# Cached keys of the samples turned by VectorE in 32x32 blocks, and loaded by quadrants in pieces of 128 bytes

## What is computed

```python
k_past = cache_k[l][page_table].reshape(dec_batch, past_len, N_KV_HEADS, HEAD_DIM)
k_all = jnp.concatenate([k_past.astype(k.dtype), k], axis=1)
...
qg = q.astype(F32).reshape(b, t, N_KV_HEADS, N_HEADS // N_KV_HEADS, HEAD_DIM)
s = jnp.einsum('btkgd,btnkd->btkgn', qg, kg) * (HEAD_DIM ** -0.5)
p = jax.nn.softmax(s, axis=-1)
o = jnp.einsum('btkgn,btnkd->btkgd', p, vg)
```

## Time and profile before

| | us |
|---|---|
| median of 3 runs | 3478.99 |
| the three runs | 3478.44, 3482.11, 3478.99 |
| span of the profiled execution | 3480.9 |
| PE busy | 3402.1 (98%) |
| POOL busy | 1224.1 (35%) |
| DVE busy | 1815.1 (52%) |
| ACT busy | 1058.5 (30%) |
| mean granted TensorE clock | 0.992 |

### The profile page before, as it was taken

The page is one execution under the profiler, slowest core; times in us unless marked ns, Lnnn a source line. Parts: engine busy times, 40 slices in busy tenths (PEclk is TensorE's granted clock), DMA queues, the critical chain, the costliest instruction groups (busy, mean ns, idle before and its releaser), DMA issues. The chain is left out here.

```text
span 3480.9 us, 66517 instructions
## 1 busy us (share of the span) xinstructions
PE 3402.1 (98%) x27598; PEld 3177.2 (91%) x27598; DVE 1815.1 (52%) x2545; ACT 1058.5 (30%) x1464; POOL 1224.1 (35%) x508
## 2 busy tenths in 40 slices
PE   5899999999999999999999999999999999999999
PEld 2699989889999989998888999898999998999999
DVE  1523578979986123332325245888889841242201
ACT  2322332223542334222213222322245423332221
POOL 0243333436323223333333433334362332233433
PEclk9899999999999999999999999999999999999999
DMA  9834434656545774658895656544332257744442
GB/s 327 278 108 115 114 105 121 182 172 199 158 131 163 232 241 157 211 194 290 293 294 171 185 170 179 142 123 111 104 115 74 87 186 234 231 140 137 124 130 88
DMA packets 559562, 593.12 MB, mean 170 GB/s; under 512 B 74780, under 2 KB 524593, under 8 KB 549179
## 3 DMA queue, kind: packets, MB, share of 16 engines
q1 hardware_dynamic: 559260, 588.86, 55.4%
HBM read 546.37 MB, written 116.39 MB: 190 GB/s over the span
## 5 line engine op out<-in xcount | busy, mean ns | idle before, releaser
L858 POOL TENSOR_TENSOR w_lo_t<-raw,w_hi_t 128x1024 fp32r<-128x1024 f32 x472 | 1179.0, 2498 | 2233.5 <-ACT w_hi_t L871 2233.5
L1177 PE MATMUL acc<-act_hi,w_hi_t 128*128 128x272 f32 x6528 | 1392.6, 295 | 21.7 <-POOL w_lo_t L858 11.8
L1177 PE MATMUL acc<-act_hi,w_lo_t 128*128 128x272 f32 x6528 | 1354.1, 289 | 0.0
L1177 PE MATMUL acc<-act_lo,w_hi_t 128*128 128x272 f32 x6528 | 1350.1, 288 | 0.0
L1177 PEld LDWEIGHTS acc<-act_hi,w_hi_t 128*128 128x128 f32 x6528 | 1029.0, 189 | 92.7 <-issue 70.5
L1177 PEld LDWEIGHTS acc<-act_lo,w_hi_t 128*128 128x128 f32 x6528 | 1029.1, 189 | 0.0
L1177 PEld LDWEIGHTS acc<-act_hi,w_lo_t 128*128 128x128 f32 x6528 | 1023.5, 190 | 0.0
L871 ACT ACTIVATE w_hi_t<-raw 128x1024 fp32r<-128x1024 f32 x472 | 499.9, 1059 | 1611.2 <-PE acc L1177 1598.3
L1765 DVE SCALAR_TENSOR_TENSOR conv<-conv,cw 128x512 f32<-128x512 f32 x240 | 241.4, 1006 | 38.8 <-POOL w_lo_t L858 38.8
L1177 PE MATMUL acc<-m_hi,w_hi_t 128*128 128x272 f32 x1024 | 215.8, 292 | 0.0
L1177 PE MATMUL acc<-m_lo,w_hi_t 128*128 128x272 f32 x1024 | 211.5, 288 | 0.0
(11 more groups left out here) (248 smaller groups left out, 2623.1 us busy)
## 6 DMA issues: line engine op xcount, KB each, us to landing
raw<-in_w_in_dram SPq DMA_DIRECT2D x272, 512.0 KB, 3.8
ada_ring<-in_w_ada_dram SPq DMA_DIRECT2D x95, 512.0 KB, 7.0
raw<-in_w_in_dram SPq DMA_DIRECT2D x136, 256.0 KB, 3.3
k_near<-in_cache_k_dram SPq DMA_DIRECT2D x256, 128.0 KB, 2.7
v_near<-in_cache_v_dram SPq DMA_DIRECT2D x256, 128.0 KB, 2.7
k_ring<-k_near SPq DMA_DIRECT2D x64, 512.0 KB, 4.7
v_page<-v_near SPq DMA_DIRECT2D x64, 512.0 KB, 6.3
raw<-in_w_out_dram SPq DMA_DIRECT2D x64, 512.0 KB, 4.1
```

The costliest lines, as they stand in the source:

```text
L858: pool.tensor_tensor(w_lo_t[:, m % 2], raw[:, m % 4], w_hi_t[:, m % 2].bitcast(F32), ALU.subtract).then_inc(S.w_lo, 1)
L1177: last = pe.matmul(acc[:, 2 * m + h, 0:HALF], w[:, c % 2, k, P * m:P * m + P], r[:, kt, h * HALF:(h + 1) * HALF], start=first and k == 0 a ...
```

## The change

The turn of the keys goes from PE to DVE. DVE has an instruction that transposes each block of 32x32 within a group of 32 partitions (a quadrant). For its result to be the full transpose, the blocks must already lie in the right quadrant. So the load puts them there: quadrant a gets, for both heads, numbers 32a to 32a+31 of each key, with key 32m+k on partition k of the quadrant. One tile now takes 4 DMAs, one for each quadrant, each with 32 partitions x 2 heads x 16 groups of keys = 1024 pieces of 128 bytes. `k_ring` keeps its size and its three slots, `k_t` keeps its content. One transpose of 128x1024 on DVE then writes a tile's both heads into `k_t`. The transposes of PE, the copy by ACT and the copy by DVE are gone, and `logits_s` waits for DVE's `k_turned` alone.

```diff
+BLK = 32
-        k_ring = at(C + 16512, "k_ring", [P, 3, 4, KVW])
+        k_ring = at(C + 16512, "k_ring", [P, 3, KVH, 4 * PAGE // BLK, BLK])
@@ block.sync, load_k
-                sp.dma_start(k_ring[:, q % 3], k_near[l, b, 4 * j:4 * j + 4].rearrange("g p c -> p g c")).then_inc(k_landed[q % 3], 16)
+                rows_ = k_near[l, b, 4 * j:4 * j + 4].rearrange("a p c -> (a p) c").rearrange("(m k) (g a i) -> a k g m i", k=BLK, g=KVH, i=BLK)
+                for a in range(4):
+                    sp.dma_start(k_ring[BLK * a:BLK * a + BLK, q % 3], rows_[a]).then_inc(k_landed[q % 3], 16)
@@ block.scalar, window
-                    for j in range(4):
-                        if h == turn_at(b, j):
-                            q = 32 * l + 4 * b + j
-                            act.wait_ge(S.k_turned, q + 1)
...
-                            act.activation(k_t[:, j, 0, :], aux[:, 0, :], ACT.Copy).then_inc(S.k_cp_a, 1)
@@ block.tensor
-            def turn_k(l, b, j):
-                q = 32 * l + 4 * b + j
-                pe.wait_ge(k_landed[q % 3], 16 * (q // 3 + 1))
-                need(pe, S.k_cp_a, q)
-                need(pe, S.k_cp_b, q)
...
-                for g in range(KVH):
-                    for kk in range(4):
-                        last = pe.transpose(aux[:, g, P * kk:P * kk + P], k_ring[:, q % 3, kk, g * HD:(g + 1) * HD], ident)
-                last.then_inc(S.k_turned, 1)
             def logits_s(l, b):
-                pe.wait_ge(S.k_cp_a, 32 * l + 4 * b + 4)
-                pe.wait_ge(S.k_cp_b, 32 * l + 4 * b + 4)
+                pe.wait_ge(S.k_turned, 32 * l + 4 * b + 4)
@@ block.vector
-            def keep_k(l, b, j):
-                dve.wait_ge(S.k_turned, 32 * l + 4 * b + j + 1)
+            def turn_k(l, b, j):
+                q = 32 * l + 4 * b + j
+                dve.wait_ge(k_landed[q % 3], 64 * (q // 3 + 1))
                 if b >= 1:
                     dve.wait_ge(S.logits_s, 8 * l + b)
...
-                dve.tensor_copy(k_t[:, j, 1, :], aux[:, 1, :]).then_inc(S.k_cp_b, 1)
+                dve.transpose(k_t[:, j].rearrange("p g n -> p (g n)"), k_ring[:, q % 3].rearrange("p g m i -> p (g m i)")).then_inc(S.k_turned, 1)
```

## The result

| | before | after |
|---|---|---|
| median, us | 3480.55 (4 runs, 3478.44 to 3482.80) | 3516.14 (4 runs, 3514.70 to 3517.44) |
| span of the profiled execution | 3480.9 | 3514.9 |

The ratio is 1.0095, interval 1.0083 to 1.0107: the changed kernel is slower by 35.6 us. I had forecast 3500, 21 us slower, in a range of 3456 to 3575.

The account below looks back on a forecast made before the run. It took the DMA engines to bound the samples' attention after the change, PE's 56 us gain being lost to dearer key loads. +10.5 us a layer, +21 for both, gave 3480.9 + 21 - 1.9 = 3500, range 3456 to 3575.

Parts of the forecast that it names:

- the price of a piece: Key loads: DMA engine time for a 128-byte piece, taken as 15.5 ns, so a tile adds 2.41 us.
- straight line: Key loads: lower bound through the 1 KB and 256-byte rows, 12.3 ns for a 128-byte piece.
- my formula: Samples' attention, a layer: the sum 28 x (what a tile adds) - 56.9, zero at about 14.0 ns a piece.
- to the first logits: First key load to first logits: full DMAs delay four tiles, logits start at 1144.3 instead of 1144.07, +0.2 us.
- sequence 2: Second sequence: DMA work of 25.7 us, above PE's 23.3, so -1.1 us.
- five middle sequences: Sequences 3 to 7: DMA work of 149.0 us against 134.1 before, +14.9 us, 29.8 us for each.
- the last: Last sequence: one tile left to load, DMA work 19.0 us below PE's 23.3, so -3.5 us.
- Which wait: Middle sequences: PE waits 6.5 us each, at the logits for the last tile or at the backbone for a weight chunk.
- The clock: Rival: a 6 us wait lowers PE's clock, costing some 2.5 us each, hidden below the DMAs' 29.8; no chance given.
- Faster: Rival for key loads: cheap pieces, 12.3 ns, end at 3456; faster by over 7 us, chance 0.26.
- The rival that leads to no change: "Between", key loads: pieces of 13.5 to 14.5 ns, sum within 7 us of zero, 3479; chance 0.13.
- Dear pieces: Rival: key pieces a third above the 256-byte row, 23.3 ns, a tile adds 4.4 us, 3612; chance 0.14.

Follow-up runs that it names:

- e2: The changed kernel with the old load, one DMA of 512 pieces of 1 KB a tile, still turned by DVE: 3426.48 us.
- e1: The kernel before with only the changed kernel's loads, four DMAs of 1024 pieces of 128 bytes a tile; PE still transposes: 3518.74 us.
- e12: The changed kernel with four DMAs a tile, each of 128 pieces of 1 KB over all 128 partitions: 3430.36 us.
- e4: The changed kernel with each of a tile's four DMAs writing its 1024 pieces of 128 bytes over all 128 partitions: 3499.7 us.
- e11: The changed kernel with two DMAs a tile, each of 256 pieces of 1 KB to 64 neighbouring partitions: 3481.27 us.
- e3: The changed kernel with quadrants 1 and 3 reading the numbers of 0 and 2, so every piece begins at a multiple of 256 bytes: 3513.27 us.
- e8: The changed kernel with pieces of 256 bytes, 512 in each of a tile's four DMAs, by quadrants: 3476.92 us.
- e13: The changed kernel with k_near written by blocks in 128-byte pieces, a tile loaded by one DMA over 128 partitions, blocks in wrong quadrants: 3429.55 us.
- e5: The changed kernel with k_near written by blocks in 128-byte pieces earlier in the layer, tiles loaded by quadrants in 2 KB pieces: 3486.09 us.
- e7: The changed kernel with four DMAs a tile by quadrants, each of 128 pieces of 1 KB: 3485.28 us.
- e9: Tiles 1 and 3 of each sequence loaded and turned as in the changed kernel, tiles 0 and 2 as before: 3462.08 us.

## Why the prediction was right, and where its sizes were off

**Right.** The bound named for the changed kernel was the right one: the DMA engines, full from the first key load to the last sequence but one, beginning with the column that gave it away before the change (0.71 to 0.78 and 1.00 in the earlier trace rows). PE's gain of 0.88 us a tile is real (e2: 23.32 us a sequence), and lost (e1: without it the same time). DVE, ACT and SP carry their parts unseen: the transpose takes 1.25 us against 1.3 allowed, and the twelve more issues of a sequence cost at most 4 us in all (e12). The packets rose by 232,443, the 64 x 3584 = 229,376 forecast and what the completions of 192 more DMAs add.

**The term that was mis-sized: the price of a piece.** I took 15.5 ns, between a straight line (12.3) and the 256-byte row (17.5); 16.7 was measured. A tile adds 2.72 us and not 2.41. Put into my formula, 28 x 2.72 - 56.9 = +19.3 us for a layer; measured +17.8 and +17.2. So the sum would have held with the right price, though not its parts (below). What I lacked is a part for the destination, which I put among the rivals without a row: spread over 128 partitions a piece costs 14.5 ns (e4; 15.1 by the packets), close to what I took; the quadrant adds 1.6 to 2.2, and that is 16 of the 36 us. The Trainium skill's section on ports (SBUF — State Buffer, Door 1: The DMA port swizzle), cited at e11, bears on it; I had weighed its rule on where reads begin instead, which e3 did not bear out.

**Stretch by stretch, layer 1.**

| | forecast | measured |
|---|---|---|
| to the first logits | +0.2 | 36.85 - 34.77 = +2.1 |
| sequence 2 | -1.1 | 23.32 - 26.82 = -3.5 |
| five middle sequences | +14.9 | 153.12 - 134.11 = +19.0 |
| the last | -3.5 | 27.02 - 26.83 = +0.2 |
| sum | +10.5 | +17.8 |

- To the first logits four tiles cost 4 x 0.31 = 1.2 us more than forecast; the other 0.7 I can't put to a row.
- The middle: from the windows after, share times length is 159.9 us, where I had 149.0; over 153.12 us this is a share of 1.04. So two errors worked against each other: more work, and engines whose counted share goes to 1.04 rather than 1.00.
- Sequence 2 ran at PE's pace, better than I thought, and the last at the DMAs', worse. I had each stretch pay for the loads issued in it before. But a full queue hands its work on. With the measured price my sum gives +1.5, +0.2, +21.1 and -3.5: the errors in sequence 2 and in the last are of one size and cancel in the total, which is luck. In the last sequence of the kernel before, SP issued one tile (at 1311.13); after, three:

```profile
1321.38 7.71 SPq L623 DMA_DIRECT2D k_ring<-k_near  x4
...
1330.94 6.28 SPq L623 DMA_DIRECT2D k_ring<-k_near  x4
...
1339.61 4.00 SPq L623 DMA_DIRECT2D k_ring<-k_near  x4
```

**Which wait.** I named the last tile's logits or a weight chunk. The larger one is at the values (19.9 of 28.3 us); chunks are waited for nowhere in these sequences. It changes no term of the sum, which goes by the work in the queue.

**The clock.** The rival's size was right. From first to last logits PE loses 203.46 - 163.26 = 40.2 us against e2. It is idle for 27.1 of it (28.3 in the list of waits, of which 1.2 lie before the first logits), and 13.1 lie in matmuls at the lower clock, 1.6 to 3.2 in each of five sequences (forecast 2.5). As the DMA share stays near 1 beside it, I take this for time in which PE would have waited, as the rival said; no run tried it apart.

**The chances.** Faster had 0.26, for pieces on the straight line. No load of keys in 128-byte pieces was that cheap (14.5 ns and more, against 12.3). The rival that leads to no change hung on the alignment rule (e3) and is out. "Dear pieces" had the right mechanism, a destination of 32 partitions, and reckoned a third more: too much for pieces of 128 bytes (16.7 ns against the 15.1 of e4), too little for larger ones (28.5 against 17.5 at 256 bytes, e8 and the earlier trace rows).

**Open.** Whether a layout in which one DMA fills all 128 partitions with blocks in their right quadrants brings e13's 3430 with the keys in their places: the copies ahead would need four DMAs a page, and it was not tried. Nor is it shown why by quadrants pieces of 256 bytes and more take 1.5 to 1.7 times as long (e8; e5 against half of e13's 4 KB; the estimate at e7) and those of 128 only a tenth more.

## What to carry to other kernels

Before moving work from the busiest engine, read the DMA share of the very stretch, not of the page: with 0.75 in use, a load that takes 2.7 times as long ate the whole gain, and a full queue made the others' loads late too. Price a load by the number of its pieces and by where they go: over all 128 partitions a piece of 128 bytes took 15.1 ns where one of 256 took 17.5, so halving the pieces made a load 1.7 times as dear, and a DMA that filled only 32 or 64 partitions cost this queue more than twice as much as one that filled 128, in part by making the others' packets longer. Where the whole change tips the balance, do the part that leaves both resources just full (e9, 20.6 us gained). Small pieces can be made at a place where the DMA engines have time; that alone did not help as long as the load went by quadrants (e5), and e13, where it did, does not put the keys in their places.

## What the runs showed of the hardware that I had not expected

- 1 KB pieces to 32 partitions at a time, or to 64 neighbouring ones, cost this queue 3.68 and 3.64 us of all 16 engines a tile, against 1.60 to all 128 (e7, e11, e12); a layout of 2 KB pieces helped little (3.15, e5).
- A part of that falls on other loads: with the keys by quadrants the 1 KB packets of values and weights took 64.4 ns instead of 51.7 (e5, e13), and these loads landed in 11.9 and 11.6 us instead of 6.5 and 6.2 (e7, e12).
- For 128-byte pieces the same choice makes only 16.7 against 15.1 ns by their packets (after, e4), and whether they begin at a multiple of 256 bytes makes nothing (e3: 16.7 ns too).
- DVE's transpose of 128x1024 fp32 in 32x32 blocks takes 1.25 us, 1.22 ns a column.
- In the full queue four DMAs of 1024 pieces each take SP 7.1 us to issue (after); with room in the queue one of as many pieces, from DRAM to DRAM, takes 0.57 us (e5).
